# Copies, a split and a sigmoid in another order in the second block's mixer

## The reference

```python
def hybrid_mixer(h, w_in, ...):
    parts = jnp.split(h @ w_in, IN_OFFSETS, axis=-1)
    q_n, kc, vc, ks, vs, kw, vw, gates, q_r, k_r, v_r, g_r = parts
    o_nsa = nsa_mixer(q_n, kc, vc, ks, vs, kw, vw, gates, cmp_pe, cmp_w1, cmp_w2)
    o_ret = retention(q_r, k_r, v_r, g_r, ret_gn_g)
    return jnp.concatenate([rms_norm_2(o_nsa, nsa_out_g), o_ret], axis=-1) @ w_out

# nsa_mixer: three attentions with 8 query heads and 2 key heads of 64, joined by gates
kc = silu((kv windows of 32 positions + pe) @ w1) @ w2      # compressed keys; the same for values
s_s = q . ks - slope * distance;  p_s = masked_softmax(s_s)  # selected blocks
s_w = q . kw - slope * distance;  p_w = masked_softmax(s_w)  # window
gs = sigmoid(gates)
o = gs[0] * o_c + gs[1] * o_s + gs[2] * o_w
# retention: 4 heads of 128, scores q_r . k_r with a decay mask, times v_r
```

## Time and profile before

| | |
|---|---|
| median of 3 runs | 3415.68 us (3415.55 to 3417.55) |
| the profiled execution: its time | 3418.65 us |
| its span, first to last instruction | 3416.8 us |
| busy: TensorE, VectorE, ScalarE | 97%, 72%, 46% of the span |
| mean granted clock of TensorE | 0.987 of full speed |
| the second block's two mixers | the sixth `nin` part ends at 2257.2 us in the first; `nsv` begins at 2262.9 in the first and 2958.5 in the second |

### The profile page before, as it was taken

One profiled execution on the slowest core, in us unless ns is written; L12 is line 12 of the kernel. 1 busy time (PEld: TensorE's weight loads), 2 busy tenths in 40 slices (PEclk: granted clock), 3 DMA queues, 4 the chain that ended last, 5 costly groups with the idle time before them and its releaser, 6 DMA issues. The chain is left out here.

```text
span 3416.8 us, 50647 instructions
## 1 busy us (share of the span) xinstructions
PE 3312.6 (97%) x19990; PEld 2923.9 (86%) x19990; DVE 2452.1 (72%) x4283; ACT 1575.4 (46%) x1883; POOL 106.1 (3%) x32
## 2 busy tenths in 40 slices
PE   7999999999999999999999999998999999999998
PEld 4889999888888899998888878897878788888787
DVE  7879996778887779986667777555657575665575
ACT  4544453333335444544443345454555454544553
POOL 0014000000000041000000000000000000000000
PEclk9999999999999999999999999999999999999999
DMA  9545567778874244675666765442445455434453
GB/s 376 177 178 184 190 221 276 272 277 281 287 270 166 100 170 176 219 249 201 216 223 234 245 253 190 174 171 99 174 151 195 170 196 199 156 124 150 149 192 140
DMA packets 172163, 689.62 MB, mean 202 GB/s; under 512 B 12396, under 2 KB 78724, under 8 KB 99223
## 3 DMA queue, kind: packets, MB, share of 16 engines
q1 hardware_dynamic: 167492, 663.86, 54.4%
q10 hardware_dynamic: 4436, 22.53, 1.8%
HBM read 650.66 MB, written 35.68 MB: 201 GB/s over the span
## 5 line engine op out<-in xcount | busy, mean ns | idle before, releaser
L1494 ACT ACTIVATE weights_upper<-weights 128x2048 fp32r<-128x2048 f32 x520 | 996.0, 1916 | 1525.6 <-issue 518.9
L1998 DVE TENSOR_TENSOR weights_lower<-weights,weights_upper 128x2048 fp32r<-128x2048 f32 x498 | 1139.0, 2289 | 553.7 <-ACT weights_upper L1494 553.4
L845 PE MATMUL ps<-hT_span,weights_upper 128*128 128x256 f32 x4480 | 570.9, 285 | 1.6 <-ACT hT_span L1795 1.3
L845 PEld LDWEIGHTS ps<-hT_span,weights_upper 128*128 128x128 f32 x4480 | 550.7, 192 | 9.5 <-issue 3.9
L897 PE MATMUL ps<-hT_span,weights_upper 128*128 128x512 f32 x1664 | 396.9, 391 | 0.0
L897 PEld LDWEIGHTS ps<-hT_span,weights_upper 128*128 128x128 f32 x1664 | 305.8, 188 | 59.2
L851 PE MATMUL ps<-hT_span,weights_lower 128*128 128x256 f32 x2240 | 291.6, 283 | 0.0
L851 PEld LDWEIGHTS ps<-hT_span,weights_lower 128*128 128x128 f32 x2240 | 278.9, 192 | 0.0
L1235 PE MATMUL ps<-weights_upper,hidden_lower 128*128 128x512 f32 x1008 | 250.7, 391 | 0.0
L1235 PE MATMUL ps<-weights_upper,hidden_upper 128*128 128x512 f32 x1008 | 249.0, 389 | 0.0
L1235 PE MATMUL ps<-weights_lower,hidden_upper 128*128 128x512 f32 x1008 | 248.9, 389 | 0.0
(11 more groups left out here) (402 smaller groups left out, 3936.2 us busy)
## 6 DMA issues: line engine op xcount, KB each, us to landing
weights<-in_parts SPq DMA_DIRECT2D x264, 1024.0 KB, 4.8
weights<-in_experts SPq DMA_DIRECT2D x256, 1024.0 KB, 4.9
scr<-gates SPq DMA_DIRECT2D x32, 1024.0 KB, 8.4
work<-in_ada_s SPq DMA_DIRECT2D x96, 256.0 KB, 5.3
gates<-h SPq DMA_DIRECT2D x16, 1024.0 KB, 4.8
gates<-work SPq DMA_DIRECT2D x16, 1024.0 KB, 4.8
weights<-in_ada_w SPq DMA_DIRECT2D x6, 2048.0 KB, 15.2
scr<-in_ada_l SPq DMA_DIRECT2D x35, 256.0 KB, 5.9
```

Source lines behind the costliest of these rows:

```text
L845: m = mm(bank[:, e * T:(e + 1) * T], up[:, c, e * P:(e + 1) * P], s_[:, c, :], start=(e == 0 and n == 0 and c == 0), stop=False, skip_grou ...
L1494: f(upper[:, p_.r % SPLIT, :], raw[:, p_.r, :], ACT.Copy).then_inc(upper_ready, 1)
L1998: v.tensor_tensor(lower[:, s, :], raw[:, p_.r, :], upper[:, s, :].bitcast(F32), ALU.subtract)\
```

## The change

Four edits, all in the second block's mixer. On ScalarE the copy of bank `nin` 5 goes ahead of the upper part of `nsv` 1, and the copy of bank `ret` 3 ahead of the upper part of `rv` 1. On ScalarE the two banks of `nsv` are copied whole (280 columns), and the sigmoid of the gates reads them from SBUF behind a drain; before, it read PSUM ahead of the copies. On VectorE the positions' split moves from ahead of the maxima of the window scores to behind them. Program text of TensorE and SyncE is the same.

```diff
                 for i in range(4, 6):
                     c = 2 * (i % 2)
-                    ahead("nin", i)
+                    if i == 4:
+                        ahead("nin", i)
                     take(k, "nin", i, kk[:, c:c + 2, :])
+                ahead("nin", 5)
                 ahead("nsv", 0, 2)
                 for t in range(TT):
-                    act.wait_ge(*k.filled("nsv", t))
-                    act.sem_inc(S("held"), 1)
-                    f(stat(152 + 24 * t, 24), k.bank("nsv", t)[:, 256:280], ACT.Sigmoid)
-                for t in range(TT):
-                    f(vt2[:, t, 0:256], k.bank("nsv", t)[:, 0:256], ACT.Copy).then_inc(k.empty_sem("nsv", t), 1)
+                    take(k, "nsv", t, vt2[:, t, :], src=k.bank("nsv", t)[:, 0:280])
+                act.drain()
+                for t in range(TT):
+                    f(stat(152 + 24 * t, 24), vt2[:, t, 256:280], ACT.Sigmoid)
                 softmax_exp(near, NSA_H, 40, 56, "wmax", l + 1, "wexp")
...
+                ahead("ret", 2)
                 for i in range(2):
-                    ahead("ret", 2 + i)
                     take(k, "ret", 2 + i, kr[:, 2 * i:2 * i + 2, :])
+                ahead("ret", 3)
...
                 ahead("nin", 5)
-                v.drain()
-                v.tensor_copy(Zp2[0][:, :, :, :], Zsum)
-                v.drain()
-                v.tensor_tensor(Zp2[1][:, :, :, :], Zsum, Zp2[0][:, :, :, :].bitcast(F32), ALU.subtract)\
-                    .then_inc(S("zp"), 1)
...
                 maxima("wS", near, 24, "wmax")
+                v.tensor_copy(Zp2[0][:, :, :, :], Zsum)
+                v.drain()
+                v.tensor_tensor(Zp2[1][:, :, :, :], Zsum, Zp2[0][:, :, :, :].bitcast(F32), ALU.subtract)\
+                    .then_inc(S("zp"), 1)
                 ahead("nsv", 0, 2)
```

## The result

The changed kernel takes 3423.38 us (median of 19 runs, 3418.05 to 3428.65), the kernel before 3417.74 (19 runs): ratio 1.0016, with a 95% interval of 1.0010 to 1.0023 (intervals below are of the same kind). That is 5.6 us slower, outside the range of 3414 to 3419; the forecast was +0.5.

The account below looks back on a forecast made before the run. TensorE, busy 97% of the span, was taken as the bound, so only its waits could give time back. Per mixer +0.27 us, for two +0.54, added to the median 3415.68 gave 3416.2 us; range 3414.0 to 3419.0.

Parts of the forecast that it names:

- The maxima's net delay of 0.30: Before `nsv`: lower part 2.41 us late, split's 2.11 taken out, so maxima and TensorE's `nsv` start 0.30 later.
- The split is hidden: Behind the maxima, the split's 1.93 us fits VectorE's idle time, 2.19 in the first mixer; nobody waits.
- The sigmoid's 0.62: TensorE's 0.62 us wait before the last selection scores goes, becoming about 1.4 before `ret` 0; worth 0.
- `ret` 3: Before the retention scores: its copy, moved ahead of a weight part, starts earlier, a change of -0.03 us per mixer.
- Sum in the mixer: Per mixer: +0.30 us at `nsv`, 0 at the selection scores, -0.03 before the retention scores, together +0.27.
- the signs that I had named for a wrong prediction: Maxima starting before 2261.6, the clock of `nsv` reading 1.00, or a new wait at the exponentials or `cw1`.
- The rule weighed there: At the sigmoid: a table switch of about 2.66 us would give an estimate of +2.3 us for the two mixers.
- Two mixers: +0.54 us: Whole run: the per-mixer +0.27 us, taken for both mixers, was the full change in time.
- A further stretch at half clock: Rival, chance 0.07: the new wait before `ret` 0 brings a low-clock stretch costing 1.5 us, twice giving 3419.2.
- The three runs given: Base level of the forecast: the earlier runs' median of 3415.68 us, 3.0 lower than the profiled execution's 3418.65.
- The order works as written: Rival, chance 0.01: maxima start undelayed and TensorE goes straight to `nsv`; 4.4 us gained per mixer, 3406.8.
- ScalarE did not become the bound: Rival, chance 0.05: ScalarE bounds the retention part, costing 1.1 us per mixer with long drains, 3418.4.

Follow-up runs that it names:

- Edit 1: ScalarE's copy of `nin` 5 moved ahead of the upper part of `nsv` 1; the changed kernel without this move took 3410.61 us, ratio 0.9985 against the kernel before.
- the sigmoid alone: The kernel before with only the two `nsv` banks copied whole ahead of the sigmoid: 3418.27 us, ratio 1.0004.
- the copies alone: The kernel before with only the copies of `nin` 5 and `ret` 3 moved ahead of a weight part: 3424.47 us against 3417.67, ratio 1.0019.
- e12: The changed kernel with six added idle-filling matmuls per mixer, 2.73 us each time: 3434.35 us (5 runs), ratio 1.0045 against the kernel before.

## Why the prediction was wrong

**Right, by the profile.** Edit 1 gains nothing and delays VectorE's lower part by 2.4: lower part at 2259.53, which is 2.34 later than before once the trace's 0.13 lead is taken out. The maxima's net delay of 0.30 came as 0.36 in TensorE's start of `nsv`, with a wait of 2.41 (forecast 2.3). The split is hidden. The sigmoid's 0.62 became a wait for the maxima of 0.99 (forecast 1.4, too much: the waits that it replaces, 0.62 and 0.33, add up to 0.95, and the sigmoid alone gives 0.99 as well). `ret` 3: -0.07 (forecast -0.03). Sum in the mixer about +0.2 (forecast +0.27). None of the signs that I had named for a wrong prediction is in this trace; a fall of the clock outside the mixer was not among them. The rule weighed there, a table switch of 2.66 us on the Trainium skill's page "ScalarE: Activation LUTs" ("What ACT_TABLE_LOAD costs"), is not what this trace shows, even behind an explicit drain: copies to 2272.63, load at 2272.70 for 1.28, sigmoids at 2273.99.

**Wrong: the step from the mixer's sum to the run's time**, the sentence "Two mixers: +0.54 us" and with it the case "A further stretch at half clock" at 0.07. I carried the low-clock stretches of the profile over unchanged and looked for a new one only behind a longer wait, in the mixer. The mean clock of 0.987 says that some 45 us of full clock (0.013 of 3416.8) are missing over the whole run, many times my range. The runs show new low stretches elsewhere: in the changed kernel and its near relatives the clock falls at 2374, 2488 and 2914, behind no changed instruction. In both programs TensorE waits just ahead of each: 1.72 us before L800, 1.79 before L1432 and 2.71 before L817 in the kernel before, 2.08, 1.79 and 2.70 in the changed one, so two of the three waits are the same at either level of the clock. The low stretches make up most of the loss: of 4.4 and 6.8 us in the two profiles, the chain of the two mixers is 0.4 and less, and 0.8 is the next point. One does not always cost: in the first profile that at 2374 is made good by 2400, where a low stretch of before falls in another place, and those at 2488 and 2914 cost 1.5 and 1.6; in the second that at 2374 costs 2.0.

A delay of 0.3 us at the same place without any edit gives the same three stretches in both of its profiles; the kernel before has none in both of its own, and the sigmoid alone, a changed program with hardly a delay, has none either. So a few tenths of delay are enough to bring them in these profiles; how often they come over many runs of that delay is not shown. More delay does not bring more of them: the copies alone, 2.9 us late behind the first mixer, have none of the three. What sets the place at which they come is only argued: the time of TensorE's gaps relative to something in the clock's control, and my one forecast from that (e12) failed.

**Mis-sized: the cost of the split's move.** The stretch 2300 to 2345 lost 0.4 us or more in every kernel with the split moved (and 0.3 with the copies alone, without such a pause), and so did that from 2995 to 3045. It comes with a pause of VectorE for which the profile names no releaser:

```profile
2339.81 0.22 DVE L2748 COPY scr<-ps 128x60 f32<-128x60 f32 x1 [0.46 <-issue]
```

In the kernel before no such pause stands there. All nine profiles with the split moved have it, and one of 0.45 at the same place of the second mixer (3025.9 here); the eight others have neither. I had 0 for it; it is 0.8 us in the two mixers. Two more such pauses, of 0.56 at 2742 and 0.43 at 3224, cost TensorE nothing. Why they come there is not tried.

**The level.** The three runs given had a median of 3415.68; over 19 it is 3417.74. That is 2.1 of the 7.2 us between forecast and result.

**The other rivals.** "The order works as written" was put at 0.01 for the whole change, rightly, but its price was sound: without edit 1 it is what happens, 3.7 us per mixer against my 4.4. ScalarE did not become the bound: it waits 1.62 us for TensorE before the copy of `ret` 3.

## What to carry to other kernels

Moving a copy ahead of a weight part helps only if the copy is late against what it waits for; here it was 0.04 us behind the matmuls, and the part that was pushed back stood ahead of the next critical work on another engine (VectorE's maxima). Judge an order on all engines' queues: the same three edits without this one make the kernel 7.5 us faster. And where the clock of TensorE falls in several places of a run, a sum from one stretch has an error of several us that no term of it shows; try each version more than once and compare the low stretches of the whole run before believing a difference of 0.1 to 0.2%.

## What the runs showed of the hardware

A wait of 2.05 us before `nsv` cost 3.5 to 3.7 in all, since the matmuls behind it ran at 1.2 GHz (granted clock 0.50 at 2264; 3.66 us for 16, and 2.29 without the wait).

A delay of 0.3 us per mixer cost some 2.4 us in the run's time; one added matmul of 0.45 us per mixer, with TensorE busy, cost 3.6, and three cost 6.5. The Trainium skill's page "TensorE: Matmul & The Clock Gate" ("Part 1: The HAM clock gate") says that the number of slow matmuls of one kernel varies from run to run. The profiles agree for the part ahead of 2255 us, where two profiles of the same kernel differ by 1.3 us (the kernel before) and by 2.6 (the changed one), and for the changed kernel behind it, where one profile has a low stretch at 2488 and the other has none. The two of the kernel before agree behind 2255 to 0.3 us. No run here shows why.
